# Two parts of a memory projection moved from the attention tail into the cross-attention stages of a two-layer decoder kernel

## What is computed

```python
m, ... = _mixer(hp, ...)                  # differential attention | SSD, one output projection w_out
hp = layer_norm(ALPHA * hp + m)
mk, mv = split(mem_prompt @ w_ckv[l], 2)  # keys and values of 256 memory tokens, 4 heads of 256
q = hp @ w_cq
p = softmax(q @ mk.T / 16)                # prompt tokens against mk, decode rows against caches
hp = layer_norm(ALPHA * hp + (p @ mv) @ w_co)
hp = layer_norm(ALPHA * hp + channel(hp)) # SwiGLU (layer 0) or top-2 of 8 experts (layer 1)
```

## Time and profile before

| | us |
|---|---|
| three runs | 1763.5, 1755.17, 1757.46 (median 1757.46) |
| the profiled execution | 1755.76 |
| its span in the trace | 1753.8 |
| PE busy, matmul records | 1707.6 (97%) |
| DVE, ACT busy | 1183.2 (67%), 810.0 (46%) |
| mean granted TensorE clock | 0.99 of full speed |

### The profile page before, as it was taken

How to read it: one execution, slowest core, us unless ns; L and a number is a source line. 1 busy time by engine, 2 the same in 40 slices (tenths; PEclk the granted TensorE clock), 3 DMA queues, 4 the chain that set the end, 5 groups by cost and what they waited for, 6 DMA issues and landing times.

```text
span 1753.8 us, 22732 instructions
## 1 busy us (share of the span) xinstructions
PE 1707.6 (97%) x8473; PEld 1325.7 (76%) x8473; DVE 1183.2 (67%) x1522; ACT 810.0 (46%) x844; POOL 156.3 (9%) x141
## 2 busy tenths in 40 slices
PE   7999999899999999999989999999999999999997
PEld 4645487689999765548768888888888888888885
DVE  2687524445543358763443698888998989899986
ACT  1122211134442212221112477777777777777774
POOL 0540000000000054000001300000000000000001
PEclk9999999999999999999999899999999999999999
DMA  9566542765544446654276498999999999999993
GB/s 323 198 205 217 216 188 107 272 208 192 169 145 145 148 149 213 216 216 186 108 277 227 164 370 293 389 381 379 385 375 389 377 393 373 390 373 392 372 394 120
DMA packets 220577, 466.18 MB, mean 266 GB/s; under 512 B 11135, under 2 KB 50233, under 8 KB 220487
## 3 DMA queue, kind: packets, MB, share of 16 engines
q1 hardware_dynamic: 213446, 444.76, 70.0%
q0 software_dynamic: 4752, 16.25, 3.2%
q10 hardware_dynamic: 2304, 4.20, 0.6%
HBM read 447.10 MB, written 18.21 MB: 265 GB/s over the span
## 4 chain that ended last, share of the span: by engine, by line
PE 90%; DVE 6%; ACT 2%; issue 1%; SPq 1%; DMA 1%; ACTq 0%; DVEq 0%
PE bank L1268 87%; PE bank L1272 3%; DVE arena L2723 1%; DMA out<-mem_rows 0%; ACT arena L1884 0%; DVE R L2337 0%; DVE arena L2826 0%; DVE st L2695 0%; SPq L733 0%; ACT SQ L1905 0%; DVE pair_in L2356 0%; SPq L739 0%; ACT xT L1920 0%; DVE arena L2703 0%; DMA wr<-in_w_router 0%
## 5 line engine op out<-in xcount | busy, mean ns | idle before, releaser
L2202 DVE TENSOR_TENSOR ring_low<-ring,high 128x2048 fp32r<-128x2048 f32 x264 | 600.9, 2290 | 81.8 <-ACT high L1819 81.4
L1819 ACT ACTIVATE high<-ring 128x2048 fp32r<-128x2048 f32 x264 | 506.6, 1919 | 150.4 <-PE bank L1268 142.7
L1268 PE MATMUL bank<-high,xg_high 128*128 128x512 f32 x704 | 278.0, 395 | 0.0
L1268 PE MATMUL bank<-ring_low,xg_high 128*128 128x512 f32 x704 | 275.0, 391 | 0.0
L1268 PE MATMUL bank<-high,xg_low 128*128 128x512 f32 x704 | 274.7, 390 | 0.0
L1268 PEld LDWEIGHTS bank<-ring_low,xg_high 128*128 128x128 f32 x704 | 132.6, 188 | 28.2
L1268 PEld LDWEIGHTS bank<-high,xg_high 128*128 128x128 f32 x704 | 132.6, 188 | 27.1
L1268 PEld LDWEIGHTS bank<-high,xg_low 128*128 128x128 f32 x704 | 132.7, 189 | 26.5
L1884 ACT ACTIVATE arena<-bank 128x512 f32<-128x512 f32 (+3 forms) x89 | 43.1, 521 | 210.9 <-PE bank L1268 141.4
L1268 PE MATMUL bank<-high,he_high 128*128 128x512 f32 x352 | 139.1, 395 | 0.0
L1268 PE MATMUL bank<-ring_low,he_high 128*128 128x512 f32 x352 | 137.2, 390 | 0.0
(11 more groups left out here) (327 smaller groups left out, 2442.4 us busy)
## 6 DMA issues: line engine op xcount, KB each, us to landing
ring<-in_w_exp_gu SPq DMA_DIRECT2D x176, 1024.0 KB, 14.0
ring<-in_w_exp_down SPq DMA_DIRECT2D x40, 2048.0 KB, 16.1
ring<-in_w_in SPq DMA_DIRECT2D x12, 2048.0 KB, 11.2
ring<-in_w_ffn_gu SPq DMA_DIRECT2D x22, 1024.0 KB, 8.4
ring<-in_w_ckv SPq DMA_DIRECT2D x8, 2048.0 KB, 8.3
ring<-in_cache_mem_k SPq DMA_DIRECT2D x16, 1024.0 KB, 8.2
ring<-in_cache_mem_v SPq DMA_DIRECT2D x16, 1024.0 KB, 6.7
ring<-in_cache_attn_k SPq DMA_DIRECT2D x32, 256.0 KB, 4.3
```

The source lines that it names most:

```text
L1268: return M.matmul(out, lhsT, rhs, start=start, stop=stop)
L1819: S.activation(high_bufs[h % HIGH_BUFS][:], ring[:, s, j * HALF:(j + 1) * HALF], ACT.Copy).then_inc(split_high, 1)
L2202: V.tensor_tensor(ring_low[:, s, part], ring[:, s, part], high_bufs[h % HIGH_BUFS][:], ALU.subtract).then_inc(split_low, 1)
```

## The change

Parts 6 and 7, the second halves of the memory values, leave the attention tail, and part 5 goes where part 7 was. On PE part 6 now follows `qsT(1)`, and part 7 stands between `cPT(0,.)` and `cPT(1,.)`, where the warm-up matmuls go from eleven to three. ACT copies both parts straight into the right half of the value buffer `mem_v` and stores them from there (`late_part`, with a semaphore of its own, `late_stored`); `mem_v`'s load from HBM shrinks to the left half, and the wait for stores counts six parts. The ring's chunk `("ckv", 3)` moves behind `cq`. The order of two helper definitions changes as well.

```diff
@@ psum_groups
         add("V", "O", 0)
-        add("A", "mkv", 5)
         add("V", "oS")
-        add("A", "mkv", 6)
         add("V", "oSt")
...
         add("V", "O", 1)
-        add("A", "mkv", 7)
+        add("A", "mkv", 5)
...
             if n == 0:
                 add("V", "qsT", 1)
+                add("A", "mkv", 6)
...
         for t in range(2):
+            if t:
+                add("A", "mkv", 7)
             for kt in range(2):
                 add("A", "cPT", t, kt)
@@ ring_chunks (and the same move in SP's list of loads)
-        c += [((l, "ckv", 3), 1, "pe", (l, "mkv", 7))]
         c += [((l, "out", i), 1, "pe", (l, "m", 4 * i + 3)) for i in range(2)]
         c += [((l, "cq", i), 1, "pe", (l, "cq", 4 * i + 3)) for i in range(2)]
+        c += [((l, "ckv", 3), 1, "pe", (l, "mkv", 7))]
@@ SP
-                sp.wait_ge(mem_stored, 16 * 8 * (l + 1))
+                sp.wait_ge(mem_stored, 16 * 6 * (l + 1))
...
-                sp.dma_start(mem_v[:], o_mv[l, 0].rearrange("(t p) h d -> p t (h d)", p=P)).then_inc(mem_v_landed, 16)
+                sp.dma_start(mem_v[:, :, 0:512], o_mv[l, 0].rearrange("(t p) h d -> p t (h d)", p=P)[:, :, 0:512]
+                             ).then_inc(mem_v_landed, 16)
@@ PE
                 attend(0)
-                memory_part(5)
...
-                memory_part(6)
...
                 attend(1)
-                memory_part(7)
+                memory_part(5)
...
                     if n == 0:
                         q_rows(1)
+                        memory_part(6)
                     for b in (2 * n, 2 * n + 1):
                         q_on_all(b, 1)
                 for t in range(2):
+                    if t:
+                        memory_part(7)
                     for kt in range(2):
                         bk = turns.open(pe, (l, "cPT", t, kt))
                         if t and not kt:
-                            warm(bk, 11)
+                            warm(bk, 3)
...
                     bk = turns.open(pe, (l, "cO", i))
+                    if i == 2:
+                        copied(pe, (l, "mkv", 7))
@@ ACT
                 rms(0)
-                memory_part(5)
-                memory_part(6)
                 take_aT(1, 0)
                 take_aT(1, 1)
                 rms(1)
                 rms(2)
-                memory_part(7)
+                memory_part(5)
...
+                def late_part(t):
+
+                    part = mem_v[:, t, 512:1024]
+                    copy_out((l, "mkv", 6 + t), part, lambda bk: bk[:])
+                    copied(act, (l, "mkv", 6 + t))
+                    out = o_mv[l, 0, t * P:(t + 1) * P].rearrange("t h d -> t (h d)")
+                    act.dma_start(out[:, 512:1024], part).then_inc(late_stored, 16)
+
                 for t in range(2):
                     for hp in range(2):
                         q = 2 * t + hp
+                        if q == 1:
+                            late_part(0)
...
                 for t in range(2):
+                    if t:
+                        late_part(1)
...
+                if l == 0:
+                    act.wait_ge(late_stored, 16 * 2)
                 norm(l, 1)
@@ POOL, layer 1 and the end
+                    pool.wait_ge(late_stored, 16 * 2 * (l + 1))
...
-            pool.wait_ge(mem_stored, 16 * 8 * L)
+            pool.wait_ge(mem_stored, 16 * 6 * L)
+            pool.wait_ge(late_stored, 16 * 2 * L)
```

More of the change, by code:

```diff
@@ L607, in col_cw, with signal @@
             return vecT[:, 1, o:o + 1]
+        def signal(name, per=1):
+            return Signal(sem(name), per)
         landed = [sem(f"landed{s}") for s in range(RING)]
@@ L615, in build @@
         y_stored = sem("y_stored")
+        late_stored = sem("late_stored")
         mem_stored, mem_k_landed, mem_v_landed = sem("mem_stored"), sem("mem_k_landed"), sem("mem_v_landed")
@@ L619, in build @@
         lam_dots, setup_exps, vectors_ready = sem("lam_dots"), sem("setup_exps"), sem("vectors_ready")
-        def signal(name, per=1):
-            return Signal(sem(name), per)
         dt_abs, dt_exp, dt_exp1, dt_ln, da_ready = (
@@ L757, in _ @@
                     pages((l, "V", i), a["cache_attn_v"][l], 4 * i)
-                columns((l, "ckv", 3), a["w_ckv"][l], 512 * 3)
                 for i in range(2):
@@ L762, in _ @@
                     columns((l, "cq", i), a["w_cq"][l], 512 * i)
+                columns((l, "ckv", 3), a["w_ckv"][l], 512 * 3)
                 def request_pair(kind, i):
@@ L1993, in memory_part @@
                     c, t = divmod(i, 2)
-                    n = 8 * l + i
+                    n = 6 * l + i
                     if n >= 1:
```

## The result

The changed kernel takes **1777.23 us** (median of 5 runs, 1774.24 to 1777.62), the kernel before in the same session 1757.46 (5 runs, 1755.17 to 1763.5): ratio 1.0116, 95% interval 1.0096 to 1.0136. It is slower by 19.8 us. The profiled execution took 1777.45, its span is 1775.6; forecast was 1771, range 1761 to 1778.

A forecast was written before the change was run, and what follows sets the result against it. PE was taken to bound the kernel. Two layers losing 10.0 us each, less 5.5 won in the tails, gave +14.5: 1770.3 from the profiled 1755.76, or 1772.0 by the median; 1771 predicted, range 1761 to 1778.

The forecast's parts named there:

- the loads slip further: Rival, chance 0.10: loads at 348 GB/s and two clock dips per layer give +20.1 us, 1776 to 1778.
- Bound by PE: Whole kernel: the chain of waits runs through PE for 90% of the span, so moved matmuls cost time unless PE would wait.
- Part 6: +6.1 predicted: Cross attention: part 6 on PE ahead of the second half's first broadcast delays that broadcast by 6.1 us.
- Part 7: 2.7 predicted: Cross attention: part 7 and three warm-ups replace the wait for DVE at the weights, adding 2.7 us, +8.8 in all.
- DVE's 6.76 of waiting: Sign in cross attention: DVE should wait some 6 us more ahead of the second half's first product.
- `cPT` without a wait: Sign at the weights' transposes: the second step should follow part 7 and three warm-ups with no wait for DVE.
- backlog: Rival, chance 0.12: DVE, 6.1 us behind PE in cross attention, hides part 6; +2.3 us in all, 1758.
- The tail: Attention tails: gain of 6.9 us in layer 0 and 3.6 in layer 1, together 10.5 if PE's clock holds; 5.5 taken.
- The hole: Attention tail: PE stands idle 10.7 us ahead of oSt, waiting for DVE's eviction of the decode rows' output.
- Its clock: Behind the tail's hole: a lower PE clock costs 2.5 us per layer, between one dip and two; bounds 0 and 3.4.
- the landing of the last pair: Last decode values land at 345.8; the second half of oV waits 1.3 us, making the loss 10.0 per layer.
- estimate of +17.7: Value loads: at some 358 GB/s the last pair lands at about 347.3, each layer loses 11.6, a sum of +17.7.

The follow-up runs named there:

- e3_last: Changed kernel with the last memory quarter's later ring place, part 6 moved behind the second half's last broadcast, no warm-ups at the weights: 1770.6 us, ratio 1.0075.
- e2w_warm: Changed kernel with 23 warm-up matmuls added in PE's hole ahead of oSt, nothing else: 1770.83 us, ratio 1.0076 to the kernel before.
- e0_before: The kernel before, unchanged, run once more for a second trace: 1754.9 us.
- e7_sem: The kernel before with one more semaphore, used by nothing, which shifts the numbers of those behind it: 1756.37 us, ratio 1.0005.
- e8_semlast: Changed kernel with the semaphore late_stored defined behind all others, nothing else: 1776.93 us, ratio 1.0115 to the kernel before.
- e1_ring: Changed kernel with the last memory quarter's chunk later in the ring, behind the last pair of cached keys: 1771.4 us, ratio 1.0080 to the kernel before.
- e9_ring_again: Changed kernel with only the last memory quarter's later ring place, run again for a second trace: 1769.69 us.

## Why the prediction was right, and where it was not

The direction, the mechanism and the range held. The sum by the stages was +15.1 for +14.5 predicted, but that is luck in part: errors of both signs met (`oV` +6.6, the tails -2.4, `co` -3.4, the score stage -0.3). The measured 1777.23 lies 6 over the forecast, in the span of the rival "the loads slip further"; the loads did slip, but the tails did better than that rival had them, and what lifts the time so far is outside the stages.

- **Bound by PE:** confirmed; each moved part cost its own time less the waits and warm-ups that it took the place of. Part 6: +6.1 predicted, 309.53 - 300.41 + 0.44 - 3.43 = 6.13 measured (the 0.44 from `qsT` to part 6). Part 7: 2.7 predicted, 2.6 measured up to `cPT`'s second step. DVE's 6.76 of waiting and `cPT` without a wait came as named. No backlog hid part 6, and the other place, tried in `e3_last`, didn't hide it either.
- **The tail:** 10.5 with the clock held was predicted, 7.2 + 3.9 = 11.1 measured (`e2w_warm`). The hole is the 10.7 named. Its clock was taken as 2.5 per layer and cost 1.8 and 1.4, so the tails won 7.9 and not 5.5. But layer 0's share rested on a single trace: `e0_before` repeats its tail (38.2), while in `e7_sem`, with the same instructions, it is 3.3 shorter. The store's landing, and with it that wait, differs between traces, so 3.3 of the 7.2 are not there in every execution.
- **The step that was mis-sized: the landing of the last pair.** It was put 17.6 us behind the end of part 7, with a wait of 1.3 in `oV`. In layer 0 it came 347.35 - 326.97 = 20.4 behind, and the waits were 3.99 and 2.87, with a half clock behind the first: 5.9 and 3.1 over the two `oV`, where the prediction had 1.2 each. The 6.7 that it took for the first pair is the median of sixteen single requests of 1 MB, the longest of which took 9.3, and a pair is two of them. The windows in which these loads ran:

```profile
327.00:329.00 2.00, 2.00 (x14) 1.80 (x13) 0.00 (x0) 0.70 (x2) 0.00 (x0) 1.00 0.32 41
329.00:331.00 2.00, 1.48 (x9) 1.09 (x8) 0.96 (x3) 0.98 (x2) 0.00 (x0) 1.00 0.95 356
331.00:335.00 4.00, 4.00 (x20) 3.53 (x19) 0.00 (x0) 1.20 (x2) 0.00 (x0) 1.00 1.00 384
335.00:339.00 4.00, 3.57 (x18) 2.80 (x17) 0.49 (x2) 1.68 (x4) 0.00 (x0) 1.00 1.03 418
339.00:343.00 4.00, 3.52 (x34) 1.26 (x34) 0.23 (x1) 0.00 (x0) 0.00 (x0) 1.00 1.03 416
343.00:347.00 4.00, 0.36 (x4) 0.00 (x0) 0.00 (x0) 0.00 (x0) 0.00 (x0) 1.00 1.03 399
```

  The rate was near the 410 taken. But the windows hold 0.1 + 0.7 + 1.5 + 1.7 + 1.7 + 1.6 = 7.3 MB until then, and the three pairs with ACT's store are 6.55: the 0.7 or so above them can only be the output weights, requested at 330.73, so a transfer that was queued behind took its share before those ahead had landed. At the rate of these windows that is some 1.8 of the 2.8 us by which the pair came late, and the mean of 399 GB/s from 329 to 347 in place of 410 is another 0.4; for the rest these rows give no single cause. The Trainium skill, "DMA: Bandwidth & Descriptors", section "Where 436 GB/s comes from", says that some 358 GB/s of the HBM side bind such a load, which gave the prediction's estimate of +17.7. The trace doesn't agree with that bound as the reason: the four windows from 331 on ran at 384 to 418.
- **Not foreseen:** `co` and its norm became 1.7 shorter in both layers, as a half clock that stood there before was no longer there. -3.4 in all. In layer 0 it is not gone but stands elsewhere: the mean clock was 0.66 from 342 to 347 us before, at the start of `co`, and is 0.66 from 347 to 352 with the change, in `oV`'s second half. So the half clock behind that pause is no clear cost of the pause.
- **Outside the stages:** of the 21.8 us between the two spans, 6.7 are not in the stages, and of the 19.8 between the medians 4.7. In the traces they stand in the start (4.3) and the routing (1.8), in stretches at a lower clock that vary between executions of one program, too. `e8_semlast` shows the same total from other places. The prediction had no term for this.

## What to carry to other kernels

Before work is moved into "idle" time of another stage, add up that stage's gaps and warm-ups on the engine that bounds it, and move only as much as fits: one part fitted for 1.9 us, two cost 8.7. What is left behind has to be looked at as well: the moved work had been the cover for another engine's chain, and a bare hole costs its clock behind it, so leave one piece per wait (or warm-ups). And a weight chunk that is used later holds its ring slot longer: give it the place in the ring whose successor is needed last, which alone was worth 9.0 us over the two `oV` here, by the stages.

## What was not expected of the hardware

- A hole of 3.74 us on PE and one of 10.79 were both followed by `oSt` at 1.87 instead of 1.02: the longer hole cost no more clock than the shorter.
- The same pause in `oV` (3.99, 3.93, 2.87) was followed by a second half of 5.34, 6.22 and 3.64 us. The wait is the program's, whether and how long the clock stays low behind it is not, and time that one stage keeps is sometimes lost in another.
- Two traces of one program reach the same instruction 188 us into the span up to 3 us apart. Most stages repeat within 0.1 us, but not one that waits for a store or has a stretch at half clock in some executions (layer 0's tail before: 38.1, 38.2, 34.8; `co` of layer 0 in `e1_ring` and `e9_ring_again`: 40.0, 41.7). A single trace compares the other stages well, but not these and not ends of kernels.
